# Splitting each 512-column matmul of a two-part f32 GEMM into two 256-column ones that add into the same PSUM columns

## The reference, cut to what matters

```
h = rmsnorm(x, g_pre_mlp[l])
f = jnp.square(jax.nn.relu(jnp.einsum('bsd,df->bsf', h, w_up[l])))
f = jnp.einsum('bsf,fd->bsd', f, w_down[l])
x = x + rmsnorm(f, g_post_mlp[l])
```

## Time and profile before

| | |
|---|---|
| median of three runs | 3238.12 us |
| span of the profiled execution | 3238.2 us (0.1 us above the median) |
| TensorE matmul busy | 3031.6 us, 94% |
| TensorE weight load busy | 2629.8 us, 81% |
| VectorE busy | 2035.9 us, 63% |
| ScalarE busy | 1455.3 us, 45% |
| mean granted TensorE clock | 0.972 |
| weights moved | 479 MB at a mean of 149 GB/s |

### The profile page before, as it was taken

The page is one execution under the profiler, slowest core; times in us unless marked ns, Lnnn a source line. Parts: engine busy times, 40 slices in busy tenths (PEclk is TensorE's granted clock), DMA queues, the critical chain, the costliest instruction groups (busy, mean ns, idle before and its releaser), DMA issues.

```text
span 3238.2 us, 48155 instructions
## 1 busy us (share of the span) xinstructions
PE 3031.6 (94%) x18054; PEld 2629.8 (81%) x18054; DVE 2035.9 (63%) x2586; ACT 1455.3 (45%) x1850; POOL 3.5 (0%) x10
## 2 busy tenths in 40 slices
PE   7999999989999999989989986888986999999998
PEld 5888888868888888868779975786775888888887
DVE  4698877566465655558656657553665656666564
ACT  4445665454444444454663353223554444444443
POOL 0000000000000000000000000000000000000000
PEclk9999999989999999999999998998998999999999
DMA  5565545635565655535543320002542556566663
GB/s 172 182 193 171 176 130 169 201 106 190 185 188 183 187 188 182 187 119 171 165 140 104 105 91 1 1 1 76 165 149 73 181 189 189 191 185 193 189 189 130
DMA packets 480995, 484.64 MB, mean 150 GB/s; under 512 B 14736, under 2 KB 479632, under 8 KB 480720
## 3 DMA queue, kind: packets, MB, share of 16 engines
q1 hardware_dynamic: 480288, 479.01, 46.9%
q0 software_dynamic: 560, 3.60, 0.3%
HBM read 480.46 MB, written 2.10 MB: 149 GB/s over the span
## 4 chain that ended last, share of the span: by engine, by line
PE 45%; DVE 7%; ACT 3%; issue 1%; ACTq 0%; DVEq 0%
PE pg L371 23%; PE pg L373 12%; PE p L762 2%; PE p L751 2%; PE p L761 1%; DVE lo L308 1%; PE p L438 1%; ACT hi L272 1%; PE p L1104 1%; DVE rw_xt L804 0%; DVE rw_x L803 0%; DVE dnc L837 0%; PE pg L1371 0%; PE p L1344 0%; DVE half L466 0%
## 5 line engine op out<-in xcount | busy, mean ns | idle before, releaser
L371 PE MATMUL pg<-xa,hi 128*128 128x512 f32 x4608 | 1636.8, 400 | 43.3 <-DVE xa L455 37.0
L308 DVE TENSOR_TENSOR lo<-raw,hi 128x1024 fp32r<-128x1024 f32 x904 | 1094.5, 1224 | 835.3 <-ACT hi L272 830.3
L272 ACT ACTIVATE hi<-raw 128x1024 fp32r<-128x1024 f32 x904 | 947.2, 1058 | 1207.1 <-PE pg L373 1204.2
L373 PE MATMUL pg<-xa,lo 128*128 128x256 f32 x4608 | 1292.2, 280 | 0.0
L371 PEld LDWEIGHTS pg<-xa,hi 128*128 128x128 f32 x4608 | 872.2, 189 | 253.7 <-issue 49.2
L371 PE MATMUL pg<-xb,hi 128*128 128x512 f32 x2624 | 935.8, 401 | 15.0 <-DVE lo L308 9.6
L373 PEld LDWEIGHTS pg<-xa,lo 128*128 128x128 f32 x4608 | 875.7, 190 | 1.4 <-issue 1.2
L373 PE MATMUL pg<-xb,lo 128*128 128x256 f32 x2624 | 736.6, 281 | 0.0
L371 PEld LDWEIGHTS pg<-xb,hi 128*128 128x128 f32 x2624 | 496.9, 189 | 137.5 <-issue 11.4
L373 PEld LDWEIGHTS pg<-xb,lo 128*128 128x128 f32 x2624 | 498.7, 190 | 0.8
L282 ACT ACTIVATE half<-pg 128x512 f32<-128x512 f32 x212 | 123.6, 583 | 95.6 <-PE pg L373 95.6
(11 more groups left out here) (348 smaller groups left out, 1813.3 us busy)
## 6 DMA issues: line engine op xcount, KB each, us to landing
raw<-w_in SPq DMA_DIRECT2D x264, 512.0 KB, 4.6
raw<-ffn_w SPq DMA_DIRECT2D x256, 512.0 KB, 4.3
raw<-w_up SPq DMA_DIRECT2D x128, 512.0 KB, 3.8
raw<-w_down SPq DMA_DIRECT2D x128, 512.0 KB, 3.2
raw<-w_o SPq DMA_DIRECT2D x32, 512.0 KB, 3.6
raw<-w_out SPq DMA_DIRECT2D x32, 512.0 KB, 3.6
raw<-w_sb_out SPq DMA_DIRECT2D x16, 512.0 KB, 4.6
raw<-w_conv_out SPq DMA_DIRECT2D x16, 512.0 KB, 4.5
```

The costliest lines, as they stand in the source:

```text
L272: nc.scalar.activation(hi[:, slot], raw[:, slot], ACT.Copy).then_inc(hi_ready, 1)
L308: nc.vector.tensor_tensor(lo[:, slot], raw[:, slot], hi[:, slot].bitcast(F32), ALU.subtract).then_inc(lo_ready, 1)
L371: nc.tensor.matmul(pg[:, par, t, :], lhsT=hi[:, slot, k, c:c + P], rhs=g.x[:, kk, :], start=(j == 0 and k == 0), stop=False)
L373: ins = nc.tensor.matmul(pg[:, par, t, 0:T], lhsT=lo[:, slot, k, c:c + P], rhs=g.x[:, kk, 0:T], start=False, stop=(j == g.groups - 1 and k ...
```

## The change

Every 512-column matmul becomes two of 256 columns with the same weights: `hi` x rounded and `hi` x rest, and both, like `lo` x rounded after them, add into PSUM columns 0 to 255. The sum is then complete in one place. `take_half` goes. For "store" VectorE copies the sum out, or adds the bias (two instructions of 256 columns); for "add" and "mult" one operation takes PSUM and destination; for "relu2" ScalarE takes the ReLU from PSUM and squares it into the rounded tile, and VectorE squares on its own and subtracts.

```
-        def take_half(act, g, i, v):
+        def take_relu(act, g, i, v):
...
-            if g.bias is None:
-                nc.scalar.activation(half[:, :, :], pg[:, par, :, T:2 * T], ACT.Copy).then_inc(half_out, 1)
...
+            nc.scalar.activation(half[:, :, :], pg[:, par, :, 0:T], ACT.Relu).then_inc(relu_out, 1)
+            act.wait_ge(relu_out, own_sq)
+            nc.scalar.activation(place, half[:, :, :], ACT.Square).then_inc(rounded, 1)
...
             def block(i, v):
                 split_hi(act, g, i, v + 1, each)
-                take_half(act, g, i, v)
+                if g.kind == "relu2":
+                    take_relu(act, g, i, v)
...
+            if g.kind == "relu2":
+                own_sq = g.sq0 + t + 1
+                dve.wait_ge(relu_out, own_sq)
+                nc.vector.tensor_tensor(sq[:, :, :], half[:, :, :], half[:, :, :], ALU.mult).then_inc(squared, 1)
+                dve.wait_ge(squared, own_sq)
+                dve.wait_ge(rounded, own_sq)
+                rest = into[:, bass.ds(tile + 2 * t, 2), T:2 * T]
+                nc.vector.tensor_tensor(rest, sq[:, :, :], place.bitcast(F32), ALU.subtract).then_inc(evacuated, 1)
                 return
-            own = g.sum0 + t + 1
+            dve.wait_ge(slab_used, g.slab(i, v, g.groups - 1)[2] + 1 + RING)
             if g.kind in ("add", "mult"):
-                nc.vector.tensor_tensor(half[:, :, :], psum, half[:, :, :], ALU.add).then_inc(summed, 1)
-                dve.wait_ge(summed, own)
-                nc.vector.tensor_tensor(place, place, half[:, :, :],
-                                        ALU.add if g.kind == "add" else ALU.mult).then_inc(evacuated, 1)
...
+                nc.vector.tensor_tensor(place, psum, place, ALU.add if g.kind == "add" else ALU.mult).then_inc(evacuated, 1)
+            elif g.bias is None:
+                nc.vector.tensor_copy(place, psum).then_inc(evacuated, 1)
+            else:
+                for t_ in range(2):
+                    c = g.bias + 2 * t + t_
+                    ins = nc.vector.tensor_scalar(into[:, bass.ds(tile + 2 * t + t_, 1), off:off + T],
+                                                  pg[:, par, t_:t_ + 1, 0:T], vec[:, bass.ds(c, 1)], None, ALU.add)
+                ins.then_inc(evacuated, 1)
...
-                            nc.tensor.matmul(pg[:, par, t, :], lhsT=hi[:, slot, k, c:c + P], rhs=g.x[:, kk, :],
-                                             start=(j == 0 and k == 0), stop=False)
+                            for part in range(2):
+                                nc.tensor.matmul(pg[:, par, t, 0:T], lhsT=hi[:, slot, k, c:c + P],
+                                                 rhs=g.x[:, kk, part * T:part * T + T],
+                                                 start=(j == 0 and k == 0 and part == 0), stop=False)
```

More of the change, by code:

```diff
@@ L203, in build_program @@
         slab_used = sem("slab_used")
-        half_out = sem("half_out")
+        relu_out = sem("relu_out")
         evacuated = sem("evacuated")
-        summed = sem("summed")
         squared, rounded = sem("squared"), sem("rounded")
@@ L274, in split_hi @@
                     each()
-        def take_half(act, g, i, v):
+        def take_relu(act, g, i, v):
             b = g.b0 + i * g.unroll + v
             par = (g.b0 + v) % 2
+            own_sq = g.sq0 + i * g.unroll + v + 1
+            into, tile, off = g.dst
+            place = into[:, bass.ds(tile + 2 * (i * g.unroll + v), 2), off:off + T]
             act.wait_ge(slab_used, g.slab(i, v, g.groups - 1)[2] + 1 + RING)
             act.wait_ge(evacuated, b + 2)
-            if g.bias is None:
-                nc.scalar.activation(half[:, :, :], pg[:, par, :, T:2 * T], ACT.Copy).then_inc(half_out, 1)
[L283 to L288, removed]
+            nc.scalar.activation(half[:, :, :], pg[:, par, :, 0:T], ACT.Relu).then_inc(relu_out, 1)
+            act.wait_ge(relu_out, own_sq)
+            nc.scalar.activation(place, half[:, :, :], ACT.Square).then_inc(rounded, 1)
         def gemm_act(act, g, after=None, follows=None, each=None):
@@ L298, in gemm_act @@
             n = g.blocks - 1
-            take_half(act, g, n // g.unroll, n % g.unroll)
+            if g.kind == "relu2":
+                take_relu(act, g, n // g.unroll, n % g.unroll)
             if after:
@@ L316, in evacuate @@
             into, tile, off = g.dst
-            dve.wait_ge(half_out, g.b0 + t + 1)
             psum = pg[:, par, :, 0:T]
             place = into[:, bass.ds(tile + 2 * t, 2), off:off + T]
-            if g.kind == "store":
-                nc.vector.tensor_tensor(place, psum, half[:, :, :], ALU.add).then_inc(evacuated, 1)
+            if g.kind == "relu2":
+                own_sq = g.sq0 + t + 1
[5 more added lines that the diff above has]
+                nc.vector.tensor_tensor(rest, sq[:, :, :], place.bitcast(F32), ALU.subtract).then_inc(evacuated, 1)
@@ L322, in evacuate @@
                 return
-            own = g.sum0 + t + 1
+            dve.wait_ge(slab_used, g.slab(i, v, g.groups - 1)[2] + 1 + RING)
             if g.kind in ("add", "mult"):
-                nc.vector.tensor_tensor(half[:, :, :], psum, half[:, :, :], ALU.add).then_inc(summed, 1)
-                dve.wait_ge(summed, own)
-                nc.vector.tensor_tensor(place, place, half[:, :, :],
-                                        ALU.add if g.kind == "add" else ALU.mult).then_inc(evacuated, 1)
-                return
@@ L330, in evacuate @@
[L330 to L337, removed]
@@ L338, in evacuate @@
-            rest = into[:, bass.ds(tile + 2 * t, 2), T:2 * T]
-            nc.vector.tensor_tensor(rest, sq[:, :, :], place.bitcast(F32), ALU.subtract).then_inc(evacuated, 1)
+                nc.vector.tensor_tensor(place, psum, place, ALU.add if g.kind == "add" else ALU.mult).then_inc(evacuated, 1)
[7 more added lines that the diff above has]
+                ins.then_inc(evacuated, 1)
```

## The result

The changed kernel takes 3293.96 us, median of three runs from 3292.85 to 3294.98, against 3238.12: 1.7% slower (ratio 1.0171, 95% interval 1.0134 to 1.0209). The forecast was 3209 us. The time is inside the stated range, on the other side of the kernel before. It lies toward the case that I had called a charge per matmul.

A forecast was written before the change was run, and what follows sets the result against it. TensorE was taken as the bound, through its 7,232 matmul pairs. The pair's 24 us, VectorE's 3 and the stage ends' 2 made 29 less: 3238.2 - 29 = 3209 us, range 3145 to 3300.

The forecast's parts named there:

- a charge per matmul: TensorE's pairs, slower rival: each added matmul costs 13 ns, 0.360 us a pair, 3322 us in full; chance 0.27.
- What bounds the kernel: Whole kernel: TensorE, busy 94% of the span, sets the time through 7,232 matmul pairs, 2,503 us.
- Part one, the pair: TensorE's large products: three 256-column steps replace 512 and 256 columns, 24 us less, bounds 91 less and 89 more.
- the middle of the first two readings: TensorE's pair, between 0.114 a step and sharing by columns: 2.5 ns less in late pairs, 5.5 in early ones.
- my first reading: TensorE's pair: three steps of 0.114 make 0.341 us, 5 ns less than late pairs and 11 less than early ones.
- the sign that I had named for a wrong model: TensorE's timeline: a distance between the two `hi` matmuls unlike the other two would show one step was no model for three.
- The upper bound of the steps: TensorE's pairs: every step at 0.120, the most a single distance shows, 0.360 a pair, 89 us more.
- Part one, the load's floor: TensorE's steps: a load and a matmul can follow each other at 0.112 us; three make 0.335, 91 us less.
- Part one, PSUM: TensorE's third matmul into the same PSUM columns: any stall is already in the 0.114 distance.
- Part two, ScalarE: ScalarE: `take_half` goes, "relu2" gets two activations of some 0.58 + 0.62 us; 5.4 us still fits an 11 us block.
- Part three, VectorE: VectorE's evacuation: mostly hidden behind TensorE, 3 us less from waits for `lo`; bounds 15 less and 8 more.
- Part four, the ends: Stage ends at five norms: ScalarE's `half` goes, about 0.4 of its 0.6 us comes through, 2 us less.

The follow-up runs named there:

- the two kernels with three steps: The changed kernel, 3293.96 us, and the kernel before with only TensorE's matmuls split, halves apart in PSUM and evacuation as before, 3309.06 us.
- the first kernel of the last experiment: Kernel before with the changed form only in `sb_out`, `w_out dn`, `mem_k` and `xa_o`, old matmul order: 3227.07 us, ratio 0.9965.
- the grouped order: Kernel before with the same matmuls reordered, in each slab eight of 512 columns with `hi`, then eight of 256 with `lo`: 3235.86 us, ratio 0.998.

## Why the prediction was wrong, point by point

**What bounds the kernel: right.** The pair decides. In 21 of 32 products the two kernels with three steps agree to 0.1 us, whatever the evacuation does.

**Part one, the pair: wrong, and this is the step that failed.** I took "the middle of the first two readings", 0.1140 and 0.1153 to 0.1173 for a step of 256 columns, and read both from a step that stands between two of 512. Three in a row take 0.120 each, and so do 64 in a row of a stretch by itself. The distances around the long matmul were no model for short ones. The pair's excess of 0.026 over its columns, which I had written down for the slower rival, was the better guide: by themselves 512 and 256 columns take 0.2267 and 0.120, 13 ns above their columns each, as that rival had it. In place of 24 us less the steps cost 71 more. The rival had 89. Its rate was right (0.360 a pair), but some products hide part of it behind other waits: the split alone added 3.4 us to each later product of the last MLP and nothing to `w_out dn`, where the recurrence sets the time. It also took 2,000 pairs as the 0.353 kind where the trace holds at least 2,520, which lose 7 ns and not 13.

One reading was off as well. In the early stretch I had 0.114 for a step from starts rounded to 0.01 us; unrounded they give 0.933 us for the eight, 0.117 each, and 1,557 pairs from 750 to 1300 us give 0.117 too. That takes some 9 of the 11 ns from the gain that my first reading saw in an early pair, but doesn't turn its sign. And the sign that I had named for a wrong model, a distance between the two `hi` matmuls that differs from the others, would have missed it: all three came out equal, at 0.120.

The upper bound of the steps was set by the same rows at 0.120. That the range held the time was still partly luck: the full charge came to 3322 by my own sum, above the range's 3300, and the time fell inside because part of the charge was hidden and the evacuation gave back three times what I had put down. The chance of 0.27 for the charge was too low. Against it I had held that the 512 columns carry more of the excess. At 0.01 us a row, over two distances that move in a pattern, this was too little to stand on.

**Part one, the load's floor: right as a floor.** 0.112 is what a f32r matmul and its load take below some 240 columns. It was no limit at 256.

**Part one, PSUM: right.** The same columns cost nothing: the split with the halves apart has the same steps.

**Part two, ScalarE: right in the MLP blocks only.** There its work is hidden, no function table is loaded, and the second activation takes 0.63 us where I had estimated 0.62. In `w_out dn` the copy wasn't hidden: with only the copy gone, that product takes some 3 us less in the one trace of it. I had put it at nothing.

**Part three, VectorE: right in kind, mis-sized.** I gave 3 us; with the 2 of part four the evacuation was to bring 5, and it brought 15. The waits for `lo` fell by 5.6. The rest is in places that the row of waits for `lo` doesn't show: the last blocks of `w_out dn`, where a VectorE instruction less gives 0.86 us a block, the norms behind "add" products, and stretches in which TensorE's clock stood at its lower level for less time. I had no term for the clock.

**Part four, the ends: wrong in its cause.** The squares at the end of the last product start no earlier (0.82 us after 0.81). They wait for TensorE's sums, a condition that I had named and discounted. The kernel without the copy in "add" products agrees: its trace shows no gain at the norms. Other norms did gain with the whole change, 2.1 us at `dn` and 2.1 in the first `w1`, more than the 0.4 that I gave each. ScalarE's copy alone doesn't bring this; the VectorE instruction less and the clock are left, and no run takes those two apart.

**What stays open.** Why an f32r matmul takes 13 ns more than its columns and a bf16 one 2.5. It isn't the changing of weights, nor the PSUM columns or banks, nor simply the number of weight columns loaded. Every added matmul brought a load with it, so a charge of the matmul and one of its load haven't been told apart. The distances in long equal stretches suggest steps of a fixed size, since 0.120, 0.113, 0.147, 0.173, 0.227, 0.347 and 0.353 all lie near multiples of 0.00667; 0.2022 (448 columns with weights of 64), 0.230, 0.1316, 0.1255 and 0.112 don't, and I have no experiment that tests it. What settles a stretch at 0.347 or 0.353 isn't found either, only that the same code runs at both.

## What to carry to other kernels

A step's cost should be read from a row of equal steps, not from one between unlike neighbours; where the kernel has none, the unexplained part of the total, shared out by instruction, is a case to be given weight. Count the matmuls, not only the columns: in these runs splitting a 512-column f32r matmul in two cost 13 ns each time, though 0.120 us is above the load's floor of 0.112. An engine's saved work is worth something only in the products where the bound engine waits for it, so a change that costs the bound engine and relieves the others belongs in those alone. When time comes back at stage ends, look at the granted clock beside the waits before giving it to either.

## What the runs showed of the hardware that I had not expected

The same instructions run at 0.3467 or 0.3533 us a pair for hundreds of pairs. The long stretch from some 700 to 1,400 us ran at 0.3533 in the trace of the kernel before (1,920 pairs) and at 0.3467 in the first kernel of the last experiment, and the one from 2,400 to 3,150 us at 0.3467 in the former (1,928 pairs) and at 0.3533 without ScalarE's copy. In the trace of the kernel before the value changes only across waits. 7,232 pairs times 6.7 ns are 48 us, room enough for the spread from 3224 to 3258. Three equal steps, the grouped order and the alternation with half loads of `lo` stay within 2 to 6 us. A smaller weight load can make a matmul slower: 512 columns took 0.2267 with 128 weight columns and 0.232 with 32.
